# Seven more 1 MB weight buffers, taken from storage that is spent by then

## The reference

```python
# first block, for each group of experts
hid = silu(einsum('td,edf->tef', t, w1[sl])) * einsum('td,edf->tef', t, w3[sl])
out = out + einsum('tef,efd->td', hid * gate[:, gi, :, None], w2[sl])

# second block
for e in range(N_EXPERTS_2):
    h = jax.nn.silu(t @ w_gate[e]) * (t @ w_up[e])
    y = y + gate_dense[:, e:e + 1] * (h @ w_down[e])
```

## Time and profile before

| | |
|---|---|
| median of 3 runs | 1676.85 us |
| profiled execution | 1679.42 us |
| its span, first to last instruction | 1676.2 us |
| TensorE busy | 1570.4 us, 94% |
| VectorE, ScalarE, POOL busy | 554.8, 342.0, 148.8 us |
| mean granted TensorE clock | 0.987 of full |
| bytes moved | 404.4 MB, mean 241 GB/s |

### The profile page before, as it was taken

How to read it: one execution, slowest core, us unless ns; L and a number is a source line. 1 busy time by engine, 2 the same in 40 slices (tenths; PEclk the granted TensorE clock), 3 DMA queues, 4 the chain that set the end, 5 groups by cost and what they waited for, 6 DMA issues and landing times.

```text
span 1676.2 us, 21651 instructions
## 1 busy us (share of the span) xinstructions
PE 1570.4 (94%) x8351; PEld 1015.5 (61%) x8351; DVE 554.8 (33%) x1144; ACT 342.0 (20%) x731; POOL 148.8 (9%) x170
## 2 busy tenths in 40 slices
PE   6899999999999999999988999989999999999986
PEld 2577777677698888855544489658543544443433
DVE  2566767766522101262212110572501111101002
ACT  2344334344321100111100111441100000000001
POOL 1323442323200000000000000000000000000000
PEclk9999999999999999999999999999999999999999
DMA  9611111111944444549999974005499999999993
GB/s 374 252 39 46 42 44 43 38 38 50 373 151 136 145 151 151 199 169 389 421 421 421 421 268 151 25 1 181 194 422 421 421 408 421 421 422 400 422 421 140
DMA packets 58861, 404.40 MB, mean 241 GB/s; under 512 B 6766, under 2 KB 6898, under 8 KB 12576
## 3 DMA queue, kind: packets, MB, share of 16 engines
q1 hardware_dynamic: 52704, 381.92, 56.8%
q0 software_dynamic: 6080, 21.39, 4.3%
HBM read 402.19 MB, written 1.10 MB: 241 GB/s over the span
## 4 chain that ended last, share of the span: by engine, by line
PE 78%; DMA 9%; DVE 7%; issue 2%; ACT 2%; POOL 1%; SPq 1%; DVEq 0%; ACTq 0%; POOLq 0%
PE bank L656 76%; DMA ring<-in_moe 6%; DMA arena<-in_moe 2%; DVE arena L1728 2%; ACT arena L1370 1%; PE bank L1121 1%; POOL arena L600 1%; DMA xc<-in_xc 0%; DVE arena L1810 0%; ACT hc L1370 0%; DMA decay_rows<-arena 0%; DVE arena L1778 0%; DVE arena L1782 0%; DVE arena L1785 0%; DVE arena L1784 0%
## 5 line engine op out<-in xcount | busy, mean ns | idle before, releaser
L656 PE MATMUL bank<-arena 128*128 128x128 f32 (+3 forms) x3000 | 482.0, 311 | 28.6 <-DVE arena L1780 15.3
L656 PE MATMUL bank<-ring,arena 128*64 128x512 f32 (+2 forms) x1608 | 459.6, 604 | 25.3 <-DMA ring<-in_moe 18.1
L656 PEld LDWEIGHTS bank<-arena 128*128 128x128 f32 (+1 forms) x3000 | 394.3, 188 | 140.3 <-issue 50.3
L1370 ACT ACTIVATE arena<-bank 128x256 f32<-128x256 f32 (+2 forms) x372 | 161.2, 447 | 1112.7 <-PE bank L656 833.9
L656 PEld LDWEIGHTS bank<-ring,arena 128*64 128x64 f32 (+2 forms) x1608 | 144.1, 137 | 243.6 <-issue 239.1
L656 PE MATMUL bank<-hc,head_w 128*128 128x512 f32 (+1 forms) x384 | 162.5, 525 | 7.0 <-DVE arena L1802 6.6
L2130 DVE TENSOR_TENSOR arena<-arena,bank 128x256 f32<-128x256 f32 x48 | 20.2, 421 | 343.4 <-ACT arena L1370 343.4
L656 PE MATMUL bank<-arena,ring 128*128 128x256 f32 x416 | 92.3, 379 | 1.2 <-DVE arena L1907 1.2
L656 PE MATMUL bank<-hc,ring 128*128 128x256 f32 x416 | 91.4, 379 | 0.0
L656 PE MATMUL bank<-o_heads,arena 128*64 128x512 f32 (+2 forms) x184 | 85.3, 608 | 1.3 <-DMA ring<-in_moe 1.3
L656 PEld LDWEIGHTS bank<-arena,ring 128*128 128x128 f32 x416 | 79.0, 190 | 12.3 <-DVE arena L1907 1.6
(11 more groups left out here) (272 smaller groups left out, 1285.4 us busy)
## 6 DMA issues: line engine op xcount, KB each, us to landing
ring<-in_moe SPq DMA_DIRECT2D x201, 1024.0 KB, 17.3
ring<-in_dense SPq DMA_DIRECT2D x62, 1024.0 KB, 7.2
o_heads<-in_moe SPq DMA_DIRECT2D x23, 1024.0 KB, 18.1
xc<-in_moe SPq DMA_DIRECT2D x22, 1024.0 KB, 17.0
arena<-in_moe SPq DMA_DIRECT2D x21, 1024.0 KB, 19.4
hc<-in_moe SPq DMA_DIRECT2D x21, 1024.0 KB, 17.2
head_w<-in_head_w POOLq DMA_DIRECT2D x27, 512.0 KB, 3.9
xc<-in_dense SPq DMA_DIRECT2D x7, 1024.0 KB, 5.0
```

Source lines behind the costliest of these rows:

```text
L656: return nc.tensor.matmul(out, lhsT, rhs_, start=start, stop=stop, **kw)
L1370: return nc.scalar.activation(out, in_, func, **kw)
```

## The change

The others are places that are dead by then: `masks` (the triangle and level masks and `ba_w`, now one tile `first_w`, from the gate layers on), `head_w` (in both mixtures), `normed` (the half `H` of `hc`, once the token rows have been turned), `routing` and `places` (two parts of `arena` with what the routing leaves behind). Some small things move out of the way: `slot_of`, `slot_in`, `combine_t`, the ranks, `pick`; "ident" and "same" stand first in the masks; the attention constants are loaded in two parts, the first 128 x 256 as before, the other 128 x 1280 once the first mixture has used `head_w` for the last time (`HEAD_W_USED`, 135 slots). The warm-up matmuls read "ident" four times in place of four masks. The new homes share semaphores that have served. The branch `every_token`, which runs only if an expert gets more tokens than its places, rebuilds `H` first. Units, steps and the order of the loads stay.

```diff
-RING = 9
+RING = 11
+SHARED_SEMS = {RING - 2: ("vec_landed", 16), RING - 1: ("xc_landed", 16), "masks": ("mats_landed", 32),
+               "head_w": ("rel_set", 1), "normed": ("bias_copied", 2),
+               "routing": ("beta_made", 1), "places": ("g_ready", 1)}
...
     joins = {RING: ("x_ctx", "modulated", 1),
              G0 // BLOCKS: ("heads", "gdn_normed", 4),
-             first + RING + 2: ("tokens", "rest_taken", 5 * KT),
-             first + RING + 3: ("squares", "norm_summed", 1),
-             second + RING + 2: ("tokens", "out2_made", KT),
-             second + RING + 3: ("squares", "ln_var", 1)}
+             G0 // BLOCKS + 1: ("masks", "gdn_normed", 4),
+             first: ("head_w", "sgu_taken", KT),
+             first + RING + 4: ("tokens", "rest_taken", 5 * KT),
+             first + RING + 5: ("squares", "norm_summed", 1),
+             first + RING + 6: ("normed", "rows_copied", 4),
+             first + RING + 11: ("routing", "slots_spread", 1),
+             first + RING + 12: ("places", "slot_rows_made", 2),
+             second + RING + 4: ("head_w", "heads_squared", 8),
+             second + RING + 5: ("tokens", "out2_made", KT),
+             second + RING + 6: ("squares", "ln_var", 1),
+             second + RING + 11: ("routing", "order_ready", 2),
+             second + RING + 12: ("places", "slot_rows_made", 4)}
...
         if n == between:
-            free = [f for f in free if f[0] not in ("tokens", "squares")]
+            head_w_used = max(used for home, used in free if home == "head_w")
+            free = [f for f in free if f[0] not in ("head_w", "tokens", "squares", "routing", "places")]
...
-        mats = sb("mats", len(MATS), P)
+        first_w = sb("first_w", len(MATS) * P + 2 * DH * KT)
+        mats = first_w[:, 0:len(MATS) * P].rearrange("p (a b) -> p a b", b=P)
...
-        one_row = sb("one_row", 1, ROWS_N)
+        one_row = sb("one_row", 1, ROWS_N - D)
+        sgu_row = arena[0:1, 6144:6144 + D]
...
-        apart = {"x_ctx": XS, "heads": o_heads[:, :, :], "tokens": y_tokens, "squares": HS}
+        landed.update({home: s[name] for home, (name, _) in SHARED_SEMS.items()})
+        apart = {"x_ctx": flat(XS), "heads": flat(o_heads[:, :, :]), "tokens": flat(y_tokens), "squares": flat(HS),
+                 "normed": flat(H), "masks": first_w[:, 2 * P:2 * P + GROUP], "head_w": hw[:, 2 * P:2 * P + GROUP],
+                 "routing": area(10240, GROUP), "places": area(14336, GROUP)}
...
                 if FREE_AT[n] > 0:
                     sp.wait_ge(slots_used, FREE_AT[n])
+                elif HOME[n] in SHARED_SEMS:
+                    sp.wait_ge(landed[HOME[n]], SHARED_SEMS[HOME[n]][1])
+                if HOME[n] == "places" and n in JOINS:
+                    sp.wait_ge(s["order_ready"], JOINS[n][2] // 2)
...
+            pool.wait_ge(s["head_free"], HEADS + 1)
+            pool.dma_start(sgu_row, t["rows"][:, 0:D]).then_inc(s["tables_landed"], 16)
             pool.wait_ge(s["residual"], 1)
             pool.dma_start(arena[:, 10752:10752 + KT * (GROUPS1 + E1 + E2)], t["router_w"]).then_inc(s["router_landed"], 16)
-            pool.dma_start(hw[:, 0:1024 + 4 * P], t["attn"]).then_inc(s["attn_landed"], 16)
+            pool.dma_start(hw[:, 0:2 * P], t["attn"][:, 0:2 * P]).then_inc(s["attn_landed"], 16)
+            pool.wait_ge(slots_used, HEAD_W_USED)
+            pool.dma_start(hw[:, 2 * P:4 * P + 1024], t["attn"][:, 2 * P:]).then_inc(s["attn_landed"], 16)
             pool.wait_ge(s["x3_ready"], KT)
...
-                    mm(bank[7][:, :], ones[:, :], mats[:, 0:4, :].rearrange("p a b -> p (a b)"))
+                    mm(bank[7][:, :].rearrange("p (a b) -> p a b", a=4), ones[:, :], times(M("ident"), 4))
...
-    nc = bacc.Bacc("TRN2", target_bir_lowering=False, num_devices=1)
+    nc = bacc.Bacc("TRN2", target_bir_lowering=False, num_devices=1, dynamic_dma_scratch_size=4096)
```

More of the change, by code:

```diff
@@ L144, in slot_table @@
         free.append((home, n + 1))
-    return order, number, landed_at, home_of, free_at, joins
-ORDER, SLOT, LANDED_AT, HOME, FREE_AT, JOINS = slot_table()
+    return order, number, landed_at, home_of, free_at, joins, head_w_used
+ORDER, SLOT, LANDED_AT, HOME, FREE_AT, JOINS, HEAD_W_USED = slot_table()
 SECOND_G = FIRST_GROUPS
@@ L167 @@
     ("g_heads", KT), ("slot", E1 // 2), ("dt_bias", DH), ("a_log", DH))
-MATS = ["ident", "tri_f", "tri_b", "same"] + [f"off{k}" for k in range(LEVELS)] + [f"pick{k}" for k in range(1, LEVELS)]
+MATS = ["ident", "same", "tri_f", "tri_b"] + [f"off{k}" for k in range(LEVELS)] + [f"pick{k}" for k in range(1, LEVELS)]
 def shape_constants():
@@ L189, in shape_constants @@
     d = (np.arange(P)[:, None, None] + P * np.arange(QT)[None, :, None]) - q[None, None, :]
-    attn = np.concatenate([before.reshape(P, -1), count(d).reshape(P, -1), after, s + t == P - 1, s < t, t + 0 * s], 1).astype(np.float32)
+    attn = np.concatenate([s < t, t + 0 * s, before.reshape(P, -1), count(d).reshape(P, -1), after, s + t == P - 1], 1).astype(np.float32)
     dist = SEQ - 1 - np.arange(BIAS_W)
@@ L406, in build @@
         attn_c = hw
[L407 to L412, removed]
+        earlier = attn_c[:, 0:P]
+        slot_numbers = attn_c[:, P:2 * P]
+        before = attn_c[:, 2 * P:2 * P + 512].rearrange("p (a n) -> p a n", a=QT)
+        count = attn_c[:, 2 * P + 512:2 * P + 1024].rearrange("p (a n) -> p a n", a=QT)
+        after = attn_c[:, 2 * P + 1024:3 * P + 1024]
+        flip = attn_c[:, 3 * P + 1024:4 * P + 1024]
         rel = o_heads[0:BUCKETS + 1, 0, 0:H2]
@@ L549, in _ @@
             pool.dma_start(ba_w[:, :, :], t["ba_w"]).then_inc(s["tables_landed"], 16)
-            pool.dma_start(one_row[0:1, 0, :], t["rows"]).then_inc(s["tables_landed"], 16)
+            pool.dma_start(one_row[0:1, 0, :], t["rows"][:, D:]).then_inc(s["tables_landed"], 16)
             load_part(0, 0)
@@ L647, in _ @@
                 pool.dma_start(bias2[:, :, qt, :], rows).then_inc(s["tables_landed"], 16)
-            pool.wait_ge(s["tables_landed"], 64 + 32)
+            pool.wait_ge(s["tables_landed"], 80 + 32)
             pool.wait_ge(s["residual"], 2 * KT + 1)
@@ L1196, in every_token @@
                 src = H if m == 0 else X
+                if m == 0:
+                    for k in range(KT):
+                        for qt in range(QT):
+                            at = (k % 2) * SEQ + qt * P
+                            ins = nc.tensor.transpose(bank[4 + k // 2][:, at:at + P], own_rows[:, qt, k * P:(k + 1) * P], M("ident"))
+                    ins.then_inc(s["all0_pe"], 1)
+                    pe.wait_ge(s["all0_act"], 4)
+                base_pe, base_act = ((1, 4), (0, 0))[m]
                 pe.sem_inc(s[f"all{m}_used"], 1)
@@ L1596, in every_token @@
                 experts, sub = (E1, E2)[m], SUBS[m]
+                base_pe = (1, 0)[m]
+                if m == 0:
+                    act.wait_ge(s["all0_pe"], 1)
+                    for i in range(4):
+                        act_fn(flat(H[:, 2 * i:2 * i + 2, :]), bank[4 + i][:, :], ACT.Copy).then_inc(s["all0_act"], 1)
                 with act.Fori(0, experts) as e:
@@ L2205, in every_token @@
                                     ALU.mult, ALU.add).then_inc(own, 1)
-                dve.wait_ge(s[f"all{m}_pe"], 6 * sub * experts + 1)
+                dve.wait_ge(s[f"all{m}_pe"], base_pe + 6 * sub * experts + 1)
             mixture(0, *route1())
```

49 lines of the change are left out of this document (25 added, 24 removed).

## The result

| | before | after |
|---|---|---|
| median of the runs made together | 1677.14 us (1676.71 to 1677.9, 4 runs) | **1651.66 us** (1650.97 to 1652.09, 4 runs) |
| ratio, 95% interval | | 0.9847 (0.983 to 0.9864) |
| span of the profiled execution | 1676.2 us | 1649.6 us |
| TensorE busy | 1570.4 us | 1566.4 us |
| bytes | 404.4 MB | 404.41 MB |

The account below looks back on a forecast made before the run. TensorE was busy 94% of the span, with 26.8 us idle for weights after the queue had stood empty earlier. Gains of 14 (first mixture) and 13.5 us (second), 27.5 off 1676.85, gave 1649.4 us, range 1643 to 1661.

Parts of the forecast that it names:

- The early lead: First mixture: all 16 fixed loads issued ahead, ranked loads from 732.9 us, queue saturated; lead 6.0 million bytes, 14.2 us.
- The constants' load, 1.6 us: Late in the first mixture: POOL's load of the attention constants' second part takes 1.6 us of a saturated queue.
- I take 14, with 12.6 and 18 as ends: First mixture's gain in us: 12.6 from earlier landings, 18 from TensorE's waits plus clock loss, 14 taken.
- the queue's 12.6: First mixture: landings come 12.6 us earlier, the 14.2 us lead less 1.6 us for the constants.
- Second mixture, 13.5 us: Landings 18.4 us earlier, of which TensorE can use 12.7 us of waits plus about 0.8; then bound by TensorE.
- The forecast's low end, 1644.4: Whole kernel: 1676.85 less 18 us for the first mixture and 14.5 for the second.
- Nothing lost elsewhere: Between the mixtures everything only shifts; the first 75 us cost 0, with 2 us as bad end.
- Waits and clock: TensorE's `in_moe` waits fall from 14.1 to about 4 and 12.7 to under 1; first mixture's two half-clock stretches go.
- Both mixtures bound by TensorE: Rival, chance 0.12: larger lead in the first mixture, no wait left, 31.5 us gained, 1645.3 us.
- Only the three early loads: Rival, chance 0.12: first mixture gains 5.9 us, ranked loads go out no faster; 18.6 us in all, 1658.3 us.
- Nothing, for want of bytes: Rival, chance 0.03: loads are bound by bytes and the holes can't be filled; 0 gained, 1676.9 us.
- Slower by POOL's queue: Rival, chance 0.03: with 4096-byte scratch POOL waits between decay-row loads, holding up masks in seven heads, 52 us; 1701 us.

Follow-up runs that it names:

- the kernels with the lead held back: Changed kernel with all its storage, SyncE running only as far ahead as before: first mixture 1667.59 us, second 1664.49, both 1679.45.
- the changed kernel's second: The changed kernel measured again with no edit: 1655.34 us, ratio 0.9862.
- the kernel with the late load: Changed kernel with the second part of the attention constants issued at the start of the second layer, not at 135 slots used: 1649.53 us.
- the executions with the old lead that took 457.5: Second mixture at 457.5 us in two profiled executions with the old lead; one is the changed kernel with only that mixture held back, median 1664.49 us.
- the kernel with the lead held back in both: Changed kernel with SyncE running only as far ahead as before in both mixtures, all else kept: 1679.45 us, ratio 1.0009.
- the small scratch alone: Kernel before the change with only the scratch of dynamic DMAs cut to 4096 bytes: 1677.53 us, ratio 1.0001.

## Why the prediction was right

The forecast was 1649.4 us in a range from 1643 to 1661; measured 1651.66, 2.3 us above it, with the mechanism that it names: the kernels with the lead held back show that the whole gain is this lead. For the profiled execution I expected 1651.9 and it took 1651.3, and that closeness is luck: the mixtures gave 25.1 us and not 27.5, but the first mixture began 1.3 us earlier, and the time exceeded the span by 1.7 us only, where it was 3.2 before, and these two made up for the difference. Step by step:

- **The early lead.** Hit. All 16 loads of fixed experts were issued by 703 us. SyncE read the order at 729.0 us (the row below), issued the first ranked load at 731.63, and the queue ran at 422 from 737 on. Slot 138 landed 186.6 - 172.7 = 13.9 us ahead of before, by the mixture's own clock, for 14.2 worked out from the bytes.

```profile
L517 SPq TENSOR_LOAD <-arena x6: 265/274/476, 729.0 to 743.4; - x6
```

VectorE's cast of the order stood 1.3 us earlier than in the earlier trace rows:

```profile
728.78 0.18 DVE L2007 CAST arena<-arena 128x26 uint32<-128x26 f32 x1
```

This is no merit of the change: the half clock in the routing lasted 3.4 us in this execution and 6.8 in the one before, and 6.8 again in the changed kernel's second.

- **The constants' load, 1.6 us.** Hit, by the kernel with the late load: 1.5 us at slot 140, 1.7 in the mixture.
- **"I take 14, with 12.6 and 18 as ends".** Here the prediction failed, by 3.1 us: 10.9, outside both ends. Two faults lie in this step. In both kernels the last landing that can hold TensorE up comes 22.8 or 22.9 us ahead of the mixture's end, that of slot 145: at 204.0 us before and 193.0 now, 11.0 earlier, and the end came 10.9 earlier. (Now TensorE reaches it 0.1 us after it has landed, since it lost the time of that wait to the half clock behind slot 143.) So landings set the end, the queue's 12.6 was the number to take and not a low end, and I gave TensorE a share of its own waits that it could not have. And 12.6 was itself 1.7 too high. The first increments of slot 151 came 12.3 us earlier, so the queue is right within 0.3; the other 1.4 is the late engine, 3.6 us behind the first for 2.2 before, for which the sum has no term.
- **Second mixture, 13.5 us.** It gave 14.2, or 12.9 by the executions with the old lead that took 457.5. The last landing came 455.0 - 437.9 = 17.1 us earlier (18.4 worked out), TensorE could use its 12.7 us of waits and 1.5 us beside them, for which I had 0.8, and 2.9 us of lead were left, where I had about 5. The two errors in the landings don't reach the time, since TensorE is the bound.
- **Nothing lost elsewhere.** Hit: 235.3 and 235.2 us between the mixtures, the heads end at 419.3 and 419.2. In the sum the terms missed in opposite directions: 3.1 too much, 0.7 too little, 27.5 against 25.1. The forecast's low end, 1644.4, counts 14.5 us for the second mixture, which nothing in the prediction works out.
- **Waits and clock.** 5.9 us where I wrote about 4, none where I wrote under 1; of the two stretches at half clock one of 3.4 us was left, and I had said both would go.

The rivals. *Both mixtures bound by TensorE*: the second is, the first isn't; its 31.5 us fall with the 5.9 us of waits. *Only the three early loads*: slot 72 landed 5.6 us earlier and slot 138 13.9, so the ranked loads gained too. *Nothing, for want of bytes*: the kernel with the lead held back in both has the same bytes and storage and 1679.45 us. The rule of the Trainium skill, "SBUF — State Buffer", section "A bandwidth-pool intuition that's wrong (but worth ruling out)", that HBM is almost always the end-to-end bottleneck, does not hold for the kernel: 25.5 us went with the same 404 MB. In the saturated stretches a transfer rate is the limit (421 GB/s before and after), though no run here shows whether it is that of HBM. *Slower by POOL's queue*: 1.0001 (0.9992 to 1.0011) with the small scratch alone.

## What to carry to other kernels

A prefetch buffer is worth what it loads in a hole ahead of a saturated stretch: multiply the missing rate by the length of the thin stretches, take off what the change adds to the queue, and the remainder is the lead; it becomes time only as far as TensorE waits in that stretch. Ask of each stage whether the lead or the waits are the smaller number, and take that one, not a value between. Where landings still set the end of a stage, even a small load on another queue shows at full price, so put it into a stretch that isn't saturated.

## What the runs showed of the hardware

**An issue can block without a semaphore.** With more free buffers SyncE ran into another limit. Before, an issue for a mixture took 0.33 us in the median and 2.25 at most; after, single ones took up to 9.0 us, and the chain counts 3% on SyncE. The first line is one form of L506 (min, median, max in ns, first and last start), the second all its loads from issue to landing:

```profile
L506 SPq DMA_DIRECT2D ring<-in_moe x163: 327/333/8998, 609.1 to 1592.2; - x163
...
DMA to landing us min/median/max: 4.7/18.9/32.8
```

The 32.8 us are those of the load whose issue took 9.0 (slot 149): they are counted from the start of the issue, and from its end 23.8 us were left. Counted in the traces, an issue began with at most 11 loads on their way (issued and not landed) in the kernel before, and with at most 12 in the changed one. Of 70 issues that took over 1 us in the changed kernel 69 began with ten or more on their way, of 281 under 0.6 us only 17; in the kernel before it is 24 of 29 and 16 of 317. So from about ten loads of 1 MB under way an issue can block, whatever buffers are free, and the kernel before touched this already. The seven more slots hold loads that have landed ahead of their use, not more loads under way. In these kernels the blocking cost nothing, as the rate stayed at 421. What other sizes of load would do was not tried.

**A load is as late as the last of 16 engines.** A packet of instructions (16 KB, 1.1 us of one engine) makes one engine about 1.5 us late, and it stays late while the queue is full; the total rate stays at 421. The landings move only when this makes the latest engine later still: with the first such packet of the saturated stretch, and again when one meets an engine that is late already, as at slot 139, from where all landings of the first mixture came 1.4 to 1.5 us later. The Trainium skill, "DMA: Bandwidth & Descriptors", section "Queues, rings and completion order", says that each DMA engine goes round between the queue rows that it has work for; the packet amid SyncE's saturated loads (6.9% of the stretch from 905 to 906 us) agrees with that.

**The clock is not the same in every execution.** In the attention the stretch at a granted clock of 0.50 (the 1.2 GHz level) around 1050 to 1066 us lasted 3.4, 13.7 and 3.4 us in three executions of the changed kernel, and the stage between the mixtures took 235.2, 240.0 and 235.2 us. Over all 13 profiled executions of this document it goes with the length of the stage: 233.9 to 235.5 us without the stretch (four), 234.7 to 235.3 with 3.4 us of it (five), 237.4 with 10.2 (two), 239.7 and 240.0 with 13.7 (two).
